# Norms by token halves between the stages of block 1, and a longer unit pipeline in block 2's attention

## What is computed

```python
for l in range(DEPTH):                       # DEPTH = 2
    mod = (silu(c) @ ada_w[l] + ada_b[l]).reshape(B, 3, 3, 1, D)
    n = _modulate(_rmsnorm(h, norm_g[l, 0]), mod[:, 0, 0], mod[:, 0, 1])
    h = h + 0.5 * mod[:, 0, 2] * _swiglu(n, ffn_w_in[l, 0], ffn_w_out[l, 0])
    n = _modulate(_rmsnorm(h, norm_g[l, 1]), mod[:, 1, 0], mod[:, 1, 1])
    z = n @ mix_w_in[l]                      # q, kv, gates, uv and two gates of the merge
    ...
    merged = sigmoid(zga) * (y_a @ proj_a[l]) + sigmoid(zgb) * (y_b @ proj_b[l])
    h = h + mod[:, 1, 2] * (merged @ w_out[l])
    n = _modulate(_rmsnorm(h, norm_g[l, 2]), mod[:, 2, 0], mod[:, 2, 1])
    h = h + 0.5 * mod[:, 2, 2] * _swiglu(n, ffn_w_in[l, 1], ffn_w_out[l, 1])
return _rmsnorm(h, final_g)
```

## Time and profile before

| | |
|---|---|
| times of three runs | 4003.18, 4005.19, 4017.94 us |
| profiled execution | 4007.77 us, span 4005.3 us |
| mean granted clock of TensorE | 0.961 |
| PE busy | 3752.1 us, 94% |
| DVE busy | 2237.2 us, 56% |
| ACT busy | 1291.3 us, 32% |
| POOL busy | 351.6 us, 9% |

### The profile page before, as it was taken

One profiled execution on the slowest core, in us unless ns is written; L12 is line 12 of the kernel. 1 busy time (PEld: TensorE's weight loads), 2 busy tenths in 40 slices (PEclk: granted clock), 3 DMA queues, 4 the chain that ended last, 5 costly groups with the idle time before them and its releaser, 6 DMA issues.

```text
span 4005.3 us, 43766 instructions
## 1 busy us (share of the span) xinstructions
PE 3752.1 (94%) x17330; PEld 2966.9 (74%) x17330; DVE 2237.2 (56%) x3503; ACT 1291.3 (32%) x1821; POOL 351.6 (9%) x340
## 2 busy tenths in 40 slices
PE   6999999999999999999999999787799878899997
PEld 5888756788888888765778878787688755477886
DVE  6554544655445544554676777777655555435444
ACT  3222343223223222344224223443322234323221
POOL 0000122000000000112000010143100011400000
PEclk9999999999999999989999999998899978999998
DMA  5443201333333333210343434334233311012221
GB/s 223 160 147 147 107 32 66 137 148 128 149 144 116 149 146 147 103 73 24 122 167 120 150 145 155 116 124 139 95 142 142 110 48 42 1 42 74 95 95 42
DMA packets 84219, 451.81 MB, mean 113 GB/s; under 512 B 10193, under 2 KB 10641, under 8 KB 47153
## 3 DMA queue, kind: packets, MB, share of 16 engines
q1 hardware_dynamic: 81936, 439.35, 29.8%
q0 software_dynamic: 2080, 9.67, 0.7%
HBM read 446.88 MB, written 2.10 MB: 112 GB/s over the span
## 4 chain that ended last, share of the span: by engine, by line
PE 81%; DVE 8%; ACT 5%; issue 5%; POOL 1%; DMA 0%; DVEq 0%; POOLq 0%; SPq 0%; ACTq 0%
PE ps L578 22%; PE ps L576 22%; PE ps L577 22%; PE ps L1151 3%; PE ps L596 2%; PE ps L1187 2%; PE ps L2123 1%; ACT WH L468 1%; DVE scrc L921 1%; PE ps L1169 1%; PE ps L818 1%; ACT Pb L2155 1%; PE ps L820 1%; POOL scr L733 1%; PE ps L819 1%
## 5 line engine op out<-in xcount | busy, mean ns | idle before, releaser
L576 PE MATMUL ps<-nH,WH 128*128 128x512 f32 x2480 | 983.6, 397 | 21.1 <-DVE nL L708 19.5
L578 PE MATMUL ps<-nH,WL 128*128 128x512 f32 x2480 | 981.7, 396 | 0.0
L577 PE MATMUL ps<-nL,WH 128*128 128x512 f32 x2480 | 977.1, 394 | 0.0
L481 DVE TENSOR_TENSOR WL<-raw,WH 128x2048 fp32r<-128x2048 f32 (+2 forms) x290 | 640.3, 2210 | 590.3 <-ACT WH L468 589.6
L468 ACT ACTIVATE WH<-raw 128x2048 fp32r<-128x2048 f32 (+2 forms) x308 | 560.9, 1824 | 676.1 <-PE ps L578 656.3
L576 PEld LDWEIGHTS ps<-nH,WH 128*128 128x128 f32 x2480 | 470.4, 190 | 138.9 <-ACT nH L692 28.0
L577 PEld LDWEIGHTS ps<-nL,WH 128*128 128x128 f32 x2480 | 470.5, 190 | 107.4 <-issue 2.0
L578 PEld LDWEIGHTS ps<-nH,WL 128*128 128x128 f32 x2480 | 470.5, 190 | 101.2
L576 PE MATMUL ps<-hH,WH 128*128 128x512 f32 x1216 | 477.7, 393 | 2.2 <-DVE h L988 2.2
L578 PE MATMUL ps<-hH,WL 128*128 128x512 f32 x1216 | 479.4, 394 | 0.0
L577 PE MATMUL ps<-hL,WH 128*128 128x512 f32 x1216 | 477.4, 393 | 0.0
(11 more groups left out here) (329 smaller groups left out, 4700.4 us busy)
## 6 DMA issues: line engine op xcount, KB each, us to landing
raw<-in_wst SPq DMA_DIRECT2D x282, 1024.0 KB, 4.8
araw<-in_ast SPq DMA_DIRECT2D x225, 512.0 KB, 5.7
raw<-in_wst SPq DMA_DIRECT2D x18, 512.0 KB, 3.3
row<-in_ast SPq DMA_DIRECT2D x15, 512.0 KB, 15.0
cw<-in_cw POOLq DMA_DIRECT2D x4, 1024.0 KB, 5.9
h<-in_xT SPq DMA_DIRECT2D x1, 2048.0 KB, 8.4
raw<-in_wst SPq DMA_DIRECT2D x8, 256.0 KB, 2.6
out<-h SPq DMA_DIRECT2D x8, 256.0 KB, 2.0
```

What stands on the lines that cost most here:

```text
L481: dve.q.tensor_tensor(M.WL[k % NW][:, 0:n], M.raw[k % NR][:, 0:n], M.WH[k % NW][:, 0:n].bitcast(F32), ALU.subtract).then_inc(*v_wlo.up(k))
L576: pe.q.matmul(to, hi[:, i, cc], xh, start=i == 0, stop=False)
L577: pe.q.matmul(to, hi[:, i, cc], xl, start=False, stop=False)
L578: t = pe.q.matmul(to, lo[:, i, cc], xh, start=False, stop=i == nk - 1)
```

## The change

At five places of block 1 (into both mixers, into the second network of layer 0 and both networks of layer 1) the end of one stage, the norm and the start of the next are written as one piece. Tokens are cut into two halves, A and B, of 256. First all 8 output tiles are made for A, then for B; a network's last two chunks are one product of 6 tiles here. While PE makes B's outputs, the other engines do A's norm, whose sum and spread stand after B's second and third output. The next stage starts with four outputs side by side, first for A; B's sum and spread stand after A's third and fifth input tile. B's norm runs beside A's products. `half_*` are the operations of a norm on one half, with the PSUM banks 6 and 7 in place of a bank from the round. The weight splits of these slots are spread differently (`network_ahead`, `output_ahead`), one row of the conditioning product more is taken ahead of the piece and the rest after it, and the mixer's first two pairs become one group of four. The warm-ups go there. The first norm of all and the norms of block 2 stay.

In block 2's attention the maximum of unit u stands ahead of the inverse of unit u-1, two small DVE instructions become one, POOL's scaling gets a second operation (plus 0.0), and the turn and the value product come one unit later, with a fourth `Pb` (the context's tile `xc` is given up earlier to make room).

The core of the diff (the ACT, POOL and network_pe/act/dve/pool parts and renamed events are left out):

```diff
-        M.Pb = [sb(ph, f"Pb{i}", [128, T]) for i in range(3)]
+        M.Pb = [sb(ph, f"Pb{i}", [128, T]) for i in range(4)]
...
+        def both_halves_pe(pe, g, group):
+            A, B = lat.half
+            for o in range(8):
+                group(pe, 0, o)
+            for o in range(8):
+                group(pe, 1, o)
+                if o == 1:
+                    half_sum_pe(pe, g + "A", A)
+                if o == 2:
+                    half_spread_pe(pe, g + "A", A)
...
+        def both_halves_dve(dve, g, update, gain, ahead):
+            A, B = lat.half
+            gA, gB = g + "A", g + "B"
+            xs = [lambda i, c=p.cols: M.h[:, i, c] for p in (A, B)]
+            gain()
+            for i in range(8):
+                update(dve, 0, i)
+                if i >= 2:
+                    half_add_dve(dve, gA, A, i - 1)
+            half_add_dve(dve, gA, A, 7)
+            for i in range(8):
+                update(dve, 1, i)
+                if i == 1:
+                    half_inverse_dve(dve, gA, A)
+                if i >= 2:
+                    half_add_dve(dve, gB, B, i - 1)
+                    half_times_dve(dve, gA, A, i - 2, xs[0])
+                if i >= 3:
+                    half_low_dve(dve, gA, A, i - 3)
+                split_dve(dve, ahead(i - 1))
+            half_add_dve(dve, gB, B, 7)
...
+            half_inverse_dve(dve, gB, B)
+            for i in range(8):
+                half_times_dve(dve, gB, B, i, xs[1])
+                if i:
+                    half_low_dve(dve, gB, B, i - 1)
+            half_low_dve(dve, gB, B, 7)
...
+        def wide_halves_pe(pe, want, n, g, names):
...
+            for x, p in enumerate(lat.half):
+                h = g + "AB"[x]
+                for i in range(nk):
+                    pe.wait_ge(*a_xhi.to(h, i))
+                    pe.wait_ge(*v_xlo.to(h, i))
+                    xh, xl = lat.nH[:, i, p.cols], lat.nL[:, i, p.cols]
+                    for j, name in enumerate(names):
...
+                        pe.q.matmul(d, hi[:, i, cc], xh, start=x == i == 0, stop=False, skip_group_check=True)
+                        pe.q.matmul(d, hi[:, i, cc], xl, start=False, stop=False, skip_group_check=True)
+                        t = pe.q.matmul(d, lo[:, i, cc], xh, start=False, stop=i == nk - 1, skip_group_check=True)
...
+                    if x == 0 and i == 2:
+                        half_sum_pe(pe, g + "B", lat.half[1])
+                    if x == 0 and i == 4:
+                        half_spread_pe(pe, g + "B", lat.half[1])
...
+            def group(pe, x, o):
...
+                parts = [(k0 + o // 4, o % 4, last - 1, f) for f in range(4)] + [(k0 + 2, o, last, f) for f in range(2)]
...
+        def network_ahead(k0):
+            return lambda o: k0 + (5 if o >= 4 else 4)
+
+        def output_ahead(k0):
+            return lambda o: k0 + 4 + (2 if o >= 4 else 1 if o >= 2 else 0)
...
+        def enter_dve(dve, l, j):
+            prev, g = stage_before(l, j), f"mix{l}" if j == 1 else f"ffn{l}{j // 2}"
+            k0 = now.dve
+            now.dve += 4 if j == 2 else 3
+            split_dve(dve, k0 + NW)
+            rows_dve(dve, rows_after(k0) + 1)
...
         def attention1_pe(pe, g, l):
-            kv_pe(pe, g, 0)
-            kv_pe(pe, g, 1)
+            wide_halves_pe(pe, "mix_w_in", 2, g, [(g, "kv", i, j) for i in range(2) for j in range(2)])
             compress_pe(pe, g, l, 0)
...
-            step_dve(dve)
+            step_dve(dve, 2)
             blocks(0)
-            step_dve(dve)
             dve.wait_ge(*ld_tab.to(l))
             key(1)
...
-            for u in range(U2 + 3):
+            for u in range(U2 + 4):
                 if u < U2:
-                    softmax2_dve(dve, u)
+                    top2_dve(dve, u)
+                if 1 <= u <= U2:
+                    inverse2_dve(dve, u - 1)
...
-            dve.q.tensor_tensor(top, m1, m2, ALU.max).then_inc(*v_st.up("s2", u, "top"))
-            dve.wait_ge(*v_st.to("s2", u, "top"))
-            dve.q.tensor_scalar(top, top, -SC, None, ALU.mult).then_inc(*v_st.up("s2", u))
+            dve.q.tensor_scalar(top, m1, m2, -SC, ALU.max, ALU.mult).then_inc(*v_st.up("s2", u))
...
-                pool.q.tensor_scalar(M.Pb[i][:, :], M.Pb[i][:, :], M.st2[:, i, 5:6], None, ALU.mult
+                pool.q.tensor_scalar(M.Pb[i][:, :], M.Pb[i][:, :], M.st2[:, i, 5:6], 0.0, ALU.mult, ALU.add
```

More of the change, by code:

```diff
@@ L329, in memory @@
     lat.N, con.N, key.N = S, C, C
+    lat.half = []
+    for x in range(2):
+        half = Space()
+        half.N, half.cols, half.stat = S // 2, slice(x * S // 2, (x + 1) * S // 2), M.banks[6 + x]
+        half.nH, half.nL, half.scr, half.rs, half.r0 = lat.nH, lat.nL, lat.scr, lat.rs, 8 * x
+        lat.half.append(half)
     return M
@@ L779, in keep_dve, with half_sum_pe, half_spread_pe @@
                     yield
+        def half_sum_pe(pe, g, p):
+            pe.wait_ge(*v_ssum.to(g, 7))
+            for j in range(p.N // 128):
+                a = p.cols.start + 128 * j
+                t = pe.q.matmul(p.stat[:, j:j + 1], p.scr[2][:, a:a + 128], M.ones[:, 0:1], start=True, stop=True)
+            t.then_inc(*mm.up(g, "sum"))
+        def half_spread_pe(pe, g, p):
+            pe.wait_ge(*v_dg.to(g))
+            pe.q.matmul(p.stat[:, 0:p.N], M.ones[:, :], p.scr[3][:, p.cols], start=True, stop=True
+                        ).then_inc(*mm.up(g, "rstd"))
@@ new lines, in network_end_pe @@
+        def network_end_pe(g):
+            k0, last = now.pe, last_chunk(NF)
+            now.pe += 3
+            def group(pe, x, o):
+                c = lat.half[x].cols
+                b, free = take(g, "O", x, o)
+                pe.wait_ge(*free)
+                parts = [(k0 + o // 4, o % 4, last - 1, f) for f in range(4)] + [(k0 + 2, o, last, f) for f in range(2)]
+                for n, (k, cb, ci, f) in enumerate(parts):
+                    pe.wait_ge(*a_whi.to(k))
+                    pe.wait_ge(*wlo(k))
+                    pe.wait_ge(*a_hhi.to(g, ci, f))
+                    pe.wait_ge(*v_hlo.to(g, ci, f))
+                    hi, lo = view(M.WH, k)[:, f, 128 * cb:128 * cb + 128], view(M.WL, k)[:, f, 128 * cb:128 * cb + 128]
+                    xh, xl = M.hH[:, ci % 2, f, c], M.hL[:, ci % 2, f, c]
+                    pe.q.matmul(b[:, 0:S // 2], hi, xh, start=n == 0, stop=False)
+                    pe.q.matmul(b[:, 0:S // 2], hi, xl, start=False, stop=False)
+                    t = pe.q.matmul(b[:, 0:S // 2], lo, xh, start=False, stop=n == 5)
+                t.then_inc(*mm.up(g, "O", x, o))
+                if x and o == 3:
+                    mm.again("slot", k0)
+                if x and o == 7:
+                    mm.again("slot", k0 + 1)
+                    mm.again("slot", k0 + 2)
+            return group
@@ new lines, in output_end_pe, with group @@
+        def output_end_pe(g):
+            k0 = now.pe
+            now.pe += 4
+            def group(pe, x, o):
+                k, c = k0 + o // 2, lat.half[x].cols
+                b, free = take(g, "O", x, o)
+                pe.wait_ge(*a_whi.to(k))
+                pe.wait_ge(*wlo(k))
+                products(pe, k, o % 2, KT, b[:, 0:S // 2], lambda i: (M.mH[:, i, c], M.mL[:, i, c]),
+                         lambda i: (a_hhi.to(g, "m", i), v_hlo.to(g, "m", i)), (g, "O", x, o), free)
+                if x and o % 2:
+                    mm.again("slot", k)
+            return group
```

358 lines of the change are left out of this document (248 added, 110 removed).

## The result

The changed kernel takes 3915.27 us (median of 4 runs, 3915.16 to 3919.38) against 4005.36 (4 runs, 4003.18 to 4017.94); the ratio is 0.9771, with 95% between 0.9750 and 0.9792. The forecast was 3914, from 3893 to 3942. The total is right to 1.3 us, but two of its terms are off by 12 and 13 us in opposite directions, as the trace shows. The profiled execution took 3915.16 us around a span of 3913.4.

A forecast was written before the change was run, and what follows sets the result against it. TensorE, busy 3752 of 4005 us, was taken as the bound, with only places without real products able to give time. 4007.8 - 56 (seams) - 35 (attention) = 3917, set 2.6 lower for the median: 3914, range 3893 to 3942.

The forecast's parts named there:

- Half products cost 0.235 a pair: Five seams: two half-width products cost 0.235 us against 0.229 for a full one, 8.4 us in all.
- third rival: Half products bound by their 0.19 us weight loads: 187 us more, 4101; chance 0.03 together with any other loss.
- Network seams, 9.1, 9.1 and 10.8: Three seams into a network: 9.1 us gained twice behind a mixer, 10.8 once behind a network, 29 in sum.
- stall at the mixer's end: Start of the mixer's output: the first half group waits 3.5 us for the last mL tile, 2.7 more than before.
- Is everything else covered?: Network seams: whether DVE's norm work and weight split fit beside TensorE's second-half groups and the wide group.
- Mixer seams, 11 and 17: Two seams into a mixer: 11 us gained at the first and 17 at the second, 28 together.
- wait for R: Before compress in the mixers: PE waits 10 us in the first, 5 in the second, for DVE's copies behind rows.
- The clock behind it: Mixer seams: 2 us in the first and 1 in the second added for a clock halved in the wait.
- Rival 4: Mixers: rows aren't waited for and copies start with the wide group's end, 14 us more gained, 3900; chance 0.10.
- Attention, 35: Block 2's attention: heads 14.5 us apart instead of 18.95, 31 us over 7 heads plus 4 from filling the pipeline.
- Rival 2: Attention bound by something else, clock staying at 0.91 or eviction ahead of the maximum: 35 becomes 23, 3926; chance 0.13.
- rival 1: Seams late: DVE's second-half loop slips, nL late in the wide group, each seam gives 5 us less, 3939; chance 0.12.

The follow-up runs named there:

- e12: Changed kernel with the context's last squares a step earlier, mixers' rows behind VectorE's copies, and row loads issued ahead of weight loads: 3896.7 us.
- e13: Changed kernel with one edit, SyncE issuing a row's load ahead of the weight load of the same step: 3907.6 us.
- e10: Changed kernel with the context's last two squares and additions done one step earlier on ACT and VectorE: 3913.0 us.
- e9: Changed kernel with half of the work taken out of six modulation rows on VectorE at the last network's seam: 3915.2 us.
- e7: Changed kernel with POOL's scaling of Pb in block 2's attention as one operation and not two: 3918.5 us.
- e2: Changed kernel with the old attention functions of block 2: 3965.4 us.
- e5: Changed kernel with each unit's inverse again right behind its own maximum in block 2's attention, the added depth kept: 3954.2 us.

## Why the prediction came out, and where it was wrong

- **Half products cost 0.235 a pair: right.** 0.1176 apart over 60 in a row, with weight loads of 0.19 us each. The third rival (0.19 a half) is refuted, and the trace after disagrees with the sentence of the Trainium skill that was weighed there ("TensorE: Matmul & The Clock Gate", section "The mechanism", that a weight load overlaps matmuls in flight only when the row group differs): 0.1176 from start to start with loads of 0.19. The same section of the Trainium skill also lets a load be pulled ahead when it goes to the background weight buffer, which the prediction left out; no run here shows which buffer the loads use.
- **Network seams, 9.1, 9.1 and 10.8: two right, one lost.** Measured 10.2, 0.5 and 11.0. The sums, the spread, the norm by halves and the stall at the mixer's end came as worked out (0.86 and 2.12 us of waiting for mL at the first, against 3.5). The step that failed at the last network is "Is everything else covered?": I counted only the norm's own work on DVE. Behind it stand the rows which the seam doesn't issue, four in a row, and TensorE, now 11 us earlier, meets the context's squares behind them. I had read SyncE's queue for the mixers and not here. That the late loads and the place of the squares hold it is shown by `e12`, `e13` and `e10`; DVE's work alone, in `e9`, brought 1.6 us.
- **Mixer seams, 11 and 17: mechanism right, a term too small.** The wait for R was put at 10 and 5 and was 9.29 and 4.33. The clock behind it was put at 2 and 1 and cost 4.5 and 5.1. The seams gave 8.7 and 12.8. Rival 4, that the rows aren't waited for, is refuted by the waits of 2.87 and 1.30 us.
- **Attention, 35: mechanism right, size too small.** A head took 13.92 and not 14.5 (3.5 us over six). I had 14.5 for the interval to the last head too, which holds no scores: 10.38 (4 more). The filling gave 5.5, from 28.9 us between first scores and first values to 23.4, and not 4; and 2.4 came behind the last head, where the clock had been low. POOL's 0.91 us lies under the 0.98 estimated. That a time up to 2.20 changes nothing holds for the steady heads and not for the last one (`e7`).
- **Outside the edits**: 1.6 us at 50, 1.1 in mixer 0, 1.4 lost near the end. Nothing was forecast there.
- That the total of 3914 fits to 1.3 us is luck: two errors of 12 and 13 us cancel. The bounds of the parts were 42 to 70 and 23 to 46: the seams' 43 lies at the very end of its range, and the attention's 47 just outside. By the prediction's own terms three of these bounds are a little off: without its waits in the mixers (12 and 6) the seams come to 75, and 15.9 and 13.2 a head with 4 for the filling make 25 and 44. Rival 2 (attention bound by the clock) is wrong: it granted 1.00. So is rival 1: in the wide groups TensorE waited for no nL.

## What to carry to other kernels

When a stall on the bounding engine is filled, ask of every chore that used to run in its shade when it will be done now, on each engine and in each DMA queue, and not only of the work that replaces the stall. In an in-order queue, put the short load that somebody waits for ahead of the one that itself waits. And where two results are wanted one behind the other, making one early pays in full only when the next is early too.

## What the runs showed that I had not expected

- A wait on TensorE can cost much of itself again: 9.29 us of waiting in mixer 0 were followed by 4.5 us of lost clock, 4.33 in mixer 1 by 5.1.
- Equal streams differ, in part by the clock. `e2` has TensorE's instructions of the changed kernel up to block 2's attention and came to the same moment 8.0 us later (3260.87 against 3252.91), 1.3 of it by 60 us and the rest in steps of 0.4 to 1.2. At two of these steps, near 2160 and 2310, the granted clock is lower (0.88 against 0.92, 0.83 against 0.90); at one near 860 it is 1.00 in both.
- `e5` lost 12.7 us in this way, and 6.2 of them in one stretch: from 60 to 380 us its full products start 0.2333 us apart and those of the changed kernel 0.2289, at a granted clock of 1.00 and without waits in both. Why is open.
- At 49.5 us, before any edit, TensorE was granted 0.57 for 4 us in the kernel before and 1.00 in the changed one. The wait just ahead was 3.80 us in the first and 3.03 in the second:

```profile
49.50:53.50 4.00, 3.94 (x10) 3.15 (x11) 2.06 (x4) 1.63 (x2) 1.54 (x2) 0.57 0.52 217
```

```profile
49.50:53.50 4.00, 3.97 (x17) 3.30 (x18) 2.06 (x4) 1.63 (x2) 1.54 (x2) 1.00 0.52 213
```

- On POOL a scaling of 128x768 with one operation takes 2.20 us, with a second one that adds zero 0.91 (`e7` and the changed kernel).
- POOL's scale and shift of 128x256 takes 0.56 us in the context's norm and 0.77 in the halves' (80 of them), beside 512 columns in 0.77:

```profile
L931 POOL TENSOR_SCALAR scr<-scr,der,mods 128x256 f32<-128x256 f32 x80 | 61.8, 773 | 1532.9 <-DVE scr L844 1532.0
```

The trace shows what goes with it. In the 10 of the 80 beside which DVE runs none of its additions, subtractions or splits of tiles in SBUF (L827, L849, L489), POOL takes 0.55 to 0.56 us, as in the context's norm, where DVE stands idle beside it. Of the other 70, 64 take 0.66 to 0.92, the two beside a weight split 2.78, and four 0.55 to 0.56 all the same. The norm of the halves ran at 0.85 to 0.9 us a tile all the same.
